# Two modulation slabs of layer 1 move from the dense feed-forward to the mixer's tail and to the routing

## The reference, cut to what matters

```
def trunk_layer(x, cvec, l, P, hg_lower, cache):
    mod = jax.nn.silu(cvec) @ P['w_mod'][l] + P['b_mod'][l]
    mod = mod.reshape(cvec.shape[0], 1, N_MOD, D_MODEL)
    g = P['norm_g'][l]
    h = rmsnorm(x, g[0]) * (1.0 + mod[:, :, 1]) + mod[:, :, 0]
    m, ctx = token_mixers(h, l, P, hg_lower, cache)
    x = x + mod[:, :, 2] * rmsnorm(m, g[1])
    h = rmsnorm(x, g[2]) * (1.0 + mod[:, :, 4]) + mod[:, :, 3]
    if l % 2 == 0:
        f = swiglu(h, P['w_ffn_gu'][l // 2], P['w_ffn_down'][l // 2])
    else:
        f = moe(h, P['w_router'][l // 2], P['w_exp_gu'][l // 2], P['w_exp_down'][l // 2])
    x = x + mod[:, :, 5] * rmsnorm(f, g[3])
    return x, ctx
```

## Time and profile before

| | |
|---|---|
| runs | 1629.03, 1630.82, 1631.03 us; median 1630.82 |
| profiled execution: span, first to last instruction | 1628.5 us, 22233 instructions |
| profiled execution: its own time | given as its span alone; the three runs' times are 0.5 to 2.5 us above it |
| PE busy | 1559.0 us, 96% of the span |
| DVE, ACT, POOL busy | 1009.0, 809.5, 131.4 us |
| mean granted PE clock | 0.989 of full speed |
| loads of modulation slabs into `mod_slab` | 21, of 2048 KB each, median 9.1 us from issue to landing |

### The profile page before, as it was taken

How to read it: one execution, slowest core, us unless ns; L and a number is a source line. 1 busy time by engine, 2 the same in 40 slices (tenths; PEclk the granted TensorE clock), 3 DMA queues, 4 the chain that set the end, 5 groups by cost and what they waited for, 6 DMA issues and landing times.

```text
span 1628.5 us, 22233 instructions
## 1 busy us (share of the span) xinstructions
PE 1559.0 (96%) x9080; PEld 1192.4 (73%) x9080; DVE 1009.0 (62%) x990; ACT 809.5 (50%) x945; POOL 131.4 (8%) x89
## 2 busy tenths in 40 slices
PE   4999999999999999999989899999999999999997
PEld 1778888777778767888877786677777666766776
DVE  2654699655444665559966875555555556556576
ACT  4533744454333553364445665555545554455465
POOL 2100144000000020013410000000000000000000
PEclk7999999999999999999999999999999999999999
DMA  9875444378774367644435699999999999999991
GB/s 394 325 301 198 167 167 185 120 284 300 288 279 164 131 269 277 227 156 161 186 134 194 241 335 401 406 385 414 399 355 379 418 412 408 398 410 407 401 417 64
DMA packets 56280, 470.36 MB, mean 289 GB/s; under 512 B 6465, under 2 KB 6577, under 8 KB 9073
## 3 DMA queue, kind: packets, MB, share of 16 engines
q1 hardware_dynamic: 53712, 461.27, 72.7%
q0 software_dynamic: 2464, 7.63, 1.2%
HBM read 464.68 MB, written 4.19 MB: 288 GB/s over the span
## 4 chain that ended last, share of the span: by engine, by line
PE 84%; ACT 5%; DVE 5%; DMA 3%; issue 2%; POOL 0%; POOLq 0%; DVEq 0%; ACTq 0%; SPq 0%
PE ps L1313 22%; PE ps L1315 21%; PE ps L1314 21%; PE ps L1787 5%; PE ps L1805 3%; DVE ring_lo L2408 3%; ACT w_hi L977 2%; PE ps L1282 2%; PE ps L1522 1%; DMA ring<-in_w_in 1%; PE ps L1389 1%; PE ps L1424 1%; PE ps L1766 1%; DMA out<-state_out 1%; DMA ring<-in_w_mod 1%
## 5 line engine op out<-in xcount | busy, mean ns | idle before, releaser
L2408 DVE TENSOR_TENSOR ring_lo<-ring,w_hi 128x2048 fp32r<-128x2048 f32 x197 | 449.9, 2289 | 168.8 <-ACT w_hi L977 168.5
L1313 PE MATMUL ps<-ring_lo,h_both 128*128 128x512 f32 x1032 | 410.8, 398 | 0.9 <-DVE ring_lo L2323 0.6
L977 ACT ACTIVATE w_hi<-ring 128x2048 fp32r<-128x2048 f32 x197 | 375.2, 1910 | 68.9 <-PE ps L1315 64.8
L934 ACT ACTIVATE ring_lo<-ring 128x2048 fp32r<-128x2048 f32 x90 | 172.3, 1915 | 159.1 <-PE ps L1315 149.0
L2323 DVE TENSOR_TENSOR ring_lo<-ring,ring_lo 128x2048 fp32r<-128x2048 f32 x74 | 169.0, 2289 | 117.8 <-ACT ring_lo L934 117.2
L1313 PEld LDWEIGHTS ps<-ring_lo,h_both 128*128 128x128 f32 x1032 | 194.2, 188 | 50.4 <-issue 9.8
L1315 PE MATMUL ps<-ring_lo,h_both 128*128 128x512 f32 x592 | 230.8, 390 | 0.0
L1314 PE MATMUL ps<-ring_lo,h_both 128*128 128x512 f32 x592 | 230.5, 389 | 0.0
L1315 PE MATMUL ps<-w_hi,h_both 128*128 128x512 f32 x440 | 172.5, 392 | 0.0
L1314 PE MATMUL ps<-w_hi,h_both 128*128 128x512 f32 x440 | 171.9, 391 | 0.0
L1313 PE MATMUL ps<-ring_lo,act_hi 128*128 128x512 f32 x308 | 125.4, 407 | 9.1 <-DVE ring_lo L2408 7.4
(11 more groups left out here) (389 smaller groups left out, 1990.7 us busy)
## 6 DMA issues: line engine op xcount, KB each, us to landing
ring<-in_w_ff SPq DMA_DIRECT2D x297, 1024.0 KB, 7.4
ring<-in_w_in SPq DMA_DIRECT2D x36, 2048.0 KB, 8.7
u<-in_w_mod SPq DMA_DIRECT2D x21, 2048.0 KB, 9.1
ring<-in_w_br SPq DMA_DIRECT2D x6, 2048.0 KB, 8.5
ring<-in_w_o SPq DMA_DIRECT2D x4, 2048.0 KB, 7.9
ring<-in_w_mod SPq DMA_DIRECT2D x3, 2048.0 KB, 16.7
out<-state_out POOLq DMA_DIRECT2D x4, 512.0 KB, 5.8
x_sb<-in_x SPq DMA_DIRECT2D x1, 1024.0 KB, 10.5
```

The source lines that it names most:

```text
L934: A(hi, ring[s][:, half * UNIT:(half + 1) * UNIT], ACT.Copy).then_inc(mix_hi, 1)
L977: A(part_hi(p, n), ring[slab_slot(n)][:, p * UNIT:(p + 1) * UNIT], ACT.Copy).then_inc(hi_ready[p], 1)
L1313: mm(out, a_hi, b_lo, start=start, stop=False, skip_group_check=True)
L2408: V.tensor_tensor(ring_lo[slot][:, part], ring[slot][:, part], part_hi(p, n).bitcast(F32), ALU.subtract)\
```

## The change

Slabs (1,10) and (1,11), the two of layer 1's vector 5, leave group 2, which now has six slabs and six steps; each becomes a group of its own, 4 and 5. Group 4 runs in layer 1's tail on PE, between the third part of `project_last` and `turn_merged(l, 0)`; it is copied by ACT between the split of unit `MIX_UNITS - 3` and `merged_hi(l, 0)`, turned on PE after the fourth part of `project_last`, and read on DVE between `merged_lo(l, 0)` and `last_gated(l, 1)`. Group 5 takes the place of `stay_warm(10)` in the routing; it is copied by ACT after the copy of group 0's turned rows and before the squares of group 1, turned on PE as the new piece `("mod", 1)` in expert step 28, and read there by DVE, which then finishes vector 5. In the mixer of layer 1 DVE no longer does this. SP loads the two slabs after all slabs of layer 1's mixer, the first when the products of the recurrence's state are done (`hst_done`), the second when the first has been multiplied, and both ahead of the first loads of the experts.

```diff
-MOD_GROUPS = [mod_slabs(0, 0, 2), mod_slabs(0, 2, 5), mod_slabs(0, 5, 6) + mod_slabs(1, 0, 2) + mod_slabs(1, 5, 6),
-              mod_slabs(1, 2, 5)]
+MOD_GROUPS = [mod_slabs(0, 0, 2), mod_slabs(0, 2, 5), mod_slabs(0, 5, 6) + mod_slabs(1, 0, 2),
+              mod_slabs(1, 2, 5), [(1, 10)], [(1, 11)]]
...
-MIX_GROUP, FFN_GROUP = (1, 3), 2
+MIX_GROUP, FFN_GROUP, LAST_GROUPS = (1, 3), 2, (4, 5)
...
-                          (25, [("turn", 2), ("turn", 3), ("gates", 2)]),
+                          (25, [("turn", 2), ("turn", 3), ("gates", 2), ("mod", 1)]),
...
+            sp.wait_ge(hst_done, L)
+            load_mod(MOD_FROM[LAST_GROUPS[0]])
+            load_mod(MOD_FROM[LAST_GROUPS[1]])
             for s in range(SLOTS):
                 sp.wait_ge(*released(before0[s]))
...
                 mix_split(l, MIX_UNITS - 3)
+                if l:
+                    copy_mod(LAST_GROUPS[0], ps[:, 6:7, :])
                 merged_hi(l, 0)
...
                     elif l:
                         token_rows_hi(0)
+                        copy_mod(LAST_GROUPS[1], ps[:, 1:2, :])
                     squares_x(l, 2, g)
...
                 project_last(l, 1, 0)
+                if l:
+                    modulate(MOD_FROM[LAST_GROUPS[0]], LAST_GROUPS[0], (6,), 0)
                 turn_merged(l, 0)
                 project_last(l, 1, 1)
+                if l:
+                    turn_mod(LAST_GROUPS[0], 7, 0)
                 output(l, 0, 0)
...
+                elif kind == "mod":
+                    turn_mod(LAST_GROUPS[1], TURN, FS)
+                    return
...
+                        pe.wait_ge(mod_rest, L + 1)
                         gate_rows(5, 0, GU).then_inc(gb_done, 1)
...
                     router_scores(0)
-                    stay_warm(10)
+                    modulate(MOD_FROM[LAST_GROUPS[1]], LAST_GROUPS[1], (1,), 0)
                     places(0)
                     turn_rows(l, 2, (1,))
                     pe.wait_ge(pick_ready, 1)
                     pe.wait_ge(rows_hi, 2)
+                    pe.wait_ge(mod_copied, (0, *MIX_GROUP, *LAST_GROUPS).index(LAST_GROUPS[1]) + 1)
                     stay_warm(5)
...
+                    if s in PIECE_AT and PIECE_AT[s][0] == "mod":
+                        own(read_mod(LAST_GROUPS[1], TURN, FS), piece_read, piece_count("mod", 1))
+                        modulation(1, 5, 6, mod_rest, L + 1)
...
                 own(read_mod(MIX_GROUP[l], 4, 0), mod_read, l + 1)
-                if l:
-                    modulation(l, 5, 6, None, 0)
                 modulation(l, 2, 5, mod_rest, l + 1)
...
                 merged_lo(l, 0)
+                if l:
+                    own(read_mod(LAST_GROUPS[0], 7, 0), mod_read, L + 1)
                 last_gated(l, 1)
```

More of the change, by code:

```diff
@@ L578, in program, with pieces_done @@
         ALL_PIECES = len(PIECE_AT)
+        def pieces_done(*piece):
+            count = piece_count(*piece)
+            return count - (count > piece_count("mod", 1))
         def pieces_before(s):
@@ L1035, in read_piece @@
                 kind, a = piece[0:2]
-                act.wait_ge(piece_done, piece_count(*piece))
+                act.wait_ge(piece_done, pieces_done(*piece))
                 out = ps[:, TURN, FS:2 * FS]
@@ L1083, in experts @@
                         read_light()
-                    if s in PIECE_AT and PIECE_AT[s][0] != "corner":
+                    if s in PIECE_AT and PIECE_AT[s][0] not in ("corner", "mod"):
                         read_piece(PIECE_AT[s])
@@ L1107, in overflow @@
                         base = e * NFS + NFS * (E + 1)
-                        act.wait_ge(piece_done, e + (ALL_PIECES + 1))
+                        act.wait_ge(piece_done, e + ALL_PIECES)
                         A(pickT[:, 0].rearrange("p g m -> p (g m)"), ps[:, TURN, 0:2 * P], ACT.Copy)
@@ L1293, in turn_mod @@
                 else:
-                    pe.wait_ge(mod_copied, (0, *MIX_GROUP).index(group) + 1)
+                    pe.wait_ge(mod_copied, (0, *MIX_GROUP, *LAST_GROUPS).index(group) + 1)
                 pe.wait_ge(strips_ready, 1)
@@ L2479, in read_corner @@
                 _, p, b = PIECE_AT[s]
-                dve.wait_ge(piece_done, piece_count("corner", p, b))
+                dve.wait_ge(piece_done, pieces_done("corner", p, b))
                 dst, out = corner[:, b * FS:(b + 1) * FS], ps[:, TURN, FS:2 * FS]
@@ L2568, in experts @@
                     if s == REST[0]:
-                        dve.wait_ge(piece_done, piece_count("gates", 0))
+                        dve.wait_ge(piece_done, pieces_done("gates", 0))
                         choose_ranked(0, 2)
                     if s == REST[1]:
-                        dve.wait_ge(piece_done, piece_count("gates", 2))
+                        dve.wait_ge(piece_done, pieces_done("gates", 2))
                         choose_ranked(2, 1)
```

## The result

The changed kernel takes 1633.55 us (median of nine runs, 1632.52 to 1638.26) against 1629.74 us for the kernel before in the runs beside it (1628.02 to 1632.13). The ratio is 1.0025, 95% interval 1.0015 to 1.0035: 4.1 us slower, at least 2.4 and at most 5.7.

The account below looks back on a forecast made before the run. PE, busy 96% of the span, was taken as the bound, with chains of waits in tail and routing. -4.16 + 0.94 + 2.2 + 0 + 1.8 + 0.1 = +0.9 us on 1630.82 gave 1631.7 us, range 1627.3 to 1635.0.

Parts of the forecast that it names:

- The feed-forward: Two steps of the feed-forward on PE lose their slab and fall from 18.87 to 16.79 us: 4.16 us gained.
- The first slab in the tail: Its products on PE in layer 1's tail end near 854.1, inside the idle hole, and cost nothing by themselves.
- Its turn: The first slab's turn on PE in layer 1's tail is covered by nothing: +0.94 us.
- The store: Store of layer 1's recurrence state beside the first slab's load: lands in 7.5 us, +2.2 us; ends -0.7 and +3.4.
- only the store is quick: Rival: the tail's store lands as in layer 0, ACT's copy still costs: -2.0 us, 1628.8 us; chance 0.16.
- turns by packet: Engines alternate queues by packet, so the tail's store gains at most its own 3.0 us; sum at most +1.7.
- The second slab's load: On SP, the experts' first weights stand behind this load: between 0 and 1.0 us, taken as 0.
- The copy: In the routing, ACT's copy of the second slab's sums waits for PE and delays group 1's squares: +1.8 us.
- Step 28: The second slab's turn fits PE's 0.99 us idle time in expert step 28: +0.1 us, ends 0 and 1.9.
- The clock: Rival: idle holes in tail and routing halve PE's clock, 1.7 us a fall; two falls give 1635.1 us; 0.24.
- The sum with no fall of the clock or one: Case from 1629.5 us (store as long as before) to 1633.4 us (one fall of PE's clock); chance 0.50.
- two falls, or one with the longest store: Slow case: two falls of PE's clock (4.3 us), or one with the tail's longest store (3.8 us); chance 0.24.

Follow-up runs that it names:

- second trace of before: The kernel before run once more with no edit, one run, for a second trace: 1632.55 us.
- the fillers: The changed kernel with filling products in both holes, eight in the tail and nine in the routing: 1631.46 us, 1.0009 of the kernel before.

## Why the prediction was right and wrong

*The feed-forward*: -4.16 forecast, -4.18 measured. Right.

*The first slab in the tail*, by itself at no cost: right. Its load was there, and the idle time came behind it.

*Its turn*: +0.94 forecast, +0.9 measured. Right.

*The store*: the direction was right; the size was 7.5 us and came out at 8.55, +3.23 in place of +2.2, inside the bound of 3.4. Its premise was wrong. The 5.31 us of before were taken as the store's own time with nothing beside it; they are 3.0 and a code load. The price of the slab's load is therefore 5.5 us, of which 2.3 had been paid before by the code load, which in after lies elsewhere. The rival "only the store is quick" named the right doubt (5.31 beside a 3.0) and drew nothing from it. The bound that the prediction drew from turns by packet, at most the store's own time on top, is wrong as well: four stores near 8.5 us lie above twice 3.0, and none of the store's packets moved for 4.3 us. The Trainium skill (DMA: Bandwidth & Descriptors, "Queues, rings and completion order") says that an engine drains a whole packet, typically some 9 to 17 descriptors, before it turns to another queue. If what the profile counts as a packet is such a descriptor, the 147 of the window above are some 9 for each of the 16 engines, and one turn can be an engine's whole share of the load; this is an estimate from that page's figure. The late start of the store agrees with it, and no run tests it.

*The second slab's load* ahead of the experts' parts: 0 forecast. ACT took the first part 2.18 us later than before, and the chain ahead of it was 2.07 late. Right.

*The copy*: +1.8 forecast, +1.77 in the trace, 1.7 us in time when it was put behind. Right, hole of 2.8 us included (2.73).

*Step 28*: +0.1 forecast, 0.0 measured. Right.

*The clock* is the step that failed. The sum put a fall of the clock at nothing. "The sum with no fall of the clock or one" had 0.50, and two falls, or one with the longest store, 0.24; both holes fell, in both traces, and "a fall of the clock in either hole" was among the prediction's own signs of being wrong. What was held against it, the clock of 1.00 ahead of 854.83, was one execution's luck, as the second trace of before shows. The holes were foreseen at 2.9 and 2.8 us, and came as 4.05 and 2.73. The price was near: 1.7 for a fall was forecast, 2.4 and 1.36 were lost. The rival's 1635.1 us was 1.5 too high; in the traces falls that before had at 361, 911 and 1198 did not come in after, and the second trace of before has one in the tail in place of the one at 361. Two falls by the prediction's own sum lie just outside its range; to that extent it is luck that the range holds the time. No change within 0.2% had 0.66; the ratio of 1.0025 lies just beyond, and its interval reaches back over that line. The Trainium skill (TensorE: Matmul & The Clock Gate, "HAM oscillation — how this bites in real kernels") shows a loop in which waits of some 3 to 5 us for transfers send PE to half clock each time. The hole of 4.05 us in the tail agrees; the holes of 2.73 us in the routing and, in the second trace of before, 2.51 us in the tail are shorter and had a fall too.

The 2.8 us between the two traces are thus the terms as measured (+1.7 without the clock) and two falls, less what others gave back. Over the runs the change costs 4.1 us. The trace of before was one with a low clock for that kernel, 0.989 against a median of 0.992 in its 28 runs beside after, so the pair of traces shows less of what the clock cost than the runs do. Open is why a fall that goes in one place often comes in another; the fillers show that it does, not when.

## What to carry to other kernels

Before a slot is called free, list what its transfer and its small copies stand ahead of: here two idle holes could hold the products, but the load took a store on the critical path from 3.0 us to 8.5, and the copy held ACT ahead of a chain. Issue the small store that is waited for ahead of the large load (here on the load's own queue), and put a copy that waits for PE behind the work that does not. When the same transfer takes different times in two places of a trace, find the packet that explains it before using either as a baseline.

## What was not expected of the hardware

A 16 KB load of PE's code, one packet on one of the 16 transfer engines, lengthened a 512 KB store by 1.8 to 2.3 us here: the bulk of the store was through in 1.4 us, and the share of one engine came late. That the code is PE's is shown by the waits in PE's program, which moved the load. The page of after counts these loads:

```profile
q8 instruction: 75, 1.23, 0.3%
```

They are 0.3% of the engines' time and were overlooked for that. Where they fall depends on how many instructions PE has had before (120 waits put into PE's program moved one out of a store, 186 moved one into each of two), so an edit far away can change a critical store by 2 us. The Trainium skill (Runtime: NRT & Kernel Launch, "Instruction fetch mechanics") says that code comes in 16 KiB blocks of 256 instructions through a queue of the sequencer's own, and calls the cost mostly hidden. The size agrees with the 16 KB packets. For a store that shares the engine the cost is not hidden (5.31 against 2.98 us).
